# Block products with the tokens in the array, and a state space as real scans of states turned back by their angles

## The reference

```python
def s5_ssm(u, ...):                      # 32 groups of 16 channels, 64 complex states each
    bu_r, bu_i = einsum(uf, bbar_r), einsum(uf, bbar_i)          # bbar = coef * b
    x = associative_scan(_complex_scan_op, (a_r, a_i, bu_r, bu_i), axis=1)   # x_t = a x_{t-1} + bu_t
    return einsum(c_re, x_r) - einsum(c_im, x_i) + d * uf
def second_block(x, ...):
    for i in range(2):
        h = mixer_sb_ssm(x) if i == 0 else mixer_dsa(x)   # 0: stick-breaking attention beside s5_ssm, glu
        x = layer_norm_2(ALPHA * x + h)                   # 1: index scores, top-k mask, attention, 16 heads
        x = layer_norm_2(ALPHA * x + square(relu(x @ w1)) @ w2)              # 1024 -> 4096 -> 1024
```

## Time and profile before

| | us |
|---|---|
| median of 3 runs | 3764.23 (3763.64 to 3775.64) |
| the profiled execution | 3755.99 |
| its span | 3754.7 |
| TensorE, VectorE, ScalarE, GpSimd busy | 2697.8, 2004.3, 722.9, 1540.9 |
| the tail (from the first transpose of stage 1) | 2820 to 3754.7 |

### The profile page before, as it was taken

The page is one execution under the profiler, slowest core; times in us unless marked ns, Lnnn a source line. Parts: engine busy times, 40 slices in busy tenths (PEclk is TensorE's granted clock), DMA queues, the critical chain, the costliest instruction groups (busy, mean ns, idle before and its releaser), DMA issues.

```text
span 3754.7 us, 35721 instructions
## 1 busy us (share of the span) xinstructions
PE 2697.8 (72%) x12920; PEld 1223.2 (33%) x12920; DVE 2004.3 (53%) x5005; ACT 722.9 (19%) x1792; POOL 1540.9 (41%) x1632
## 2 busy tenths in 40 slices
PE   7758787787556775656697476565555499999998
PEld 2213332211112321111343121111114395766755
DVE  1156577745767677875213667777745655122311
ACT  0012212211122322211311121121112121020200
POOL 0034565554776666777100367767752000000000
PEclk9869988799877887776898687768887699999999
DMA  8578898899999999999432699999985268476657
GB/s 290 192 269 297 325 368 333 334 399 397 409 409 350 381 397 372 368 409 409 150 118 79 262 355 409 409 363 409 409 339 213 90 239 288 163 281 218 248 199 260
DMA packets 357508, 1145.99 MB, mean 305 GB/s; under 512 B 33412, under 2 KB 33668, under 8 KB 356308
## 3 DMA queue, kind: packets, MB, share of 16 engines
q0 software_dynamic: 236256, 867.34, 59.9%
q1 hardware_dynamic: 120660, 276.13, 20.5%
q10 hardware_dynamic: 416, 0.23, 0.0%
HBM read 1142.43 MB, written 1.15 MB: 305 GB/s over the span
## 4 chain that ended last, share of the span: by engine, by line
PE 45%; DMA 24%; DVE 17%; ACT 5%; POOL 5%; issue 3%; SPq 0%; DVEq 0%; ACTq 0%; POOLq 0%
DMA BIG<-in_p_u_dram,IDX 11%; PE PS L1012 9%; PE PS L1078 8%; DMA BIG<-in_p_v_dram,IDX 7%; DVE BIG L1873 6%; PE PS L1301 6%; PE PS L1283 5%; POOL BIG L2250 4%; DMA WR<-in_w_mod_dram 3%; PE PS L977 3%; PE PS L1040 2%; PE PS L1178 2%; PE PS L1272 2%; PE PS L988 1%; ACT dg L1468 1%
## 5 line engine op out<-in xcount | busy, mean ns | idle before, releaser
L1078 PE MATMUL PS<-BIG,dg 64*64 64x512 f32 x6144 | 1005.0, 784 | 669.0 <-DMA BIG<-in_p_v_dram,IDX 424.5
L2250 POOL DMA_INDIRECT BIG<-in_p_u_dram,IDX x768 | 737.7, 961 | 980.1 <-ACT PS L1455 463.1
L1873 DVE CUSTOM_DVE_ANT_0 BIG<-BIG,PS 128x1024 f32<-128x1024 f32 x768 | 930.3, 1216 | 322.3 <-DMA BIG<-in_p_u_dram,IDX 317.2
L2250 POOL DMA_INDIRECT BIG<-in_p_v_dram,IDX x768 | 734.3, 956 | 307.6 <-issue 136.0
L1078 PEld LDWEIGHTS PS<-BIG,dg 64*64 64x64 f32 x6144 | 263.0, 164 | 1327.9 <-issue 854.3
L1012 PE MATMUL PS<-WR,HT 128*128 128x512 f32 x640 | 300.9, 623 | 11.4 <-DMA WR<-in_b_w_in_dram 6.1
L1468 ACT ACTIVATE dg<-twin,ACTV 128x64 f32<-128x64 f32 x768 | 207.9, 336 | 330.0 <-PE PS L1078 220.7
L1283 PE MATMUL PS<-HT,WR 128*128 128x128 f32 x2048 | 258.3, 287 | 8.4 <-DMA WR<-in_mlp_w_dram 5.0
L1283 PEld LDWEIGHTS PS<-HT,WR 128*128 128x128 f32 x2048 | 248.1, 201 | 18.0 <-issue 6.2
L1301 PE MATMUL PS<-WR,BIG 128*128 128x512 f32 x512 | 227.3, 598 | 0.0
L977 PE MATMUL PS<-WR,scS 128*2 128x512 f32 x384 | 179.1, 620 | 38.9 <-DMA WR<-in_w_mod_dram 38.6
(11 more groups left out here) (295 smaller groups left out, 2730.8 us busy)
## 6 DMA issues: line engine op xcount, KB each, us to landing
WR<-in_mlp_w_dram SPq DMA_DIRECT2D x128, 1024.0 KB, 6.1
WR<-in_w_mod_dram SPq DMA_DIRECT2D x48, 1024.0 KB, 11.1
WR<-in_b_w_in_dram SPq DMA_DIRECT2D x18, 1024.0 KB, 9.6
WR<-in_a_w_in_dram SPq DMA_DIRECT2D x16, 1024.0 KB, 11.0
WR<-in_p_w_q_dram SPq DMA_DIRECT2D x16, 1024.0 KB, 9.4
BIG<-in_sb_ssm_w_in_dram POOLq DMA_DIRECT2D x16, 1024.0 KB, 7.5
BIG<-in_dsa_w_dram POOLq DMA_DIRECT2D x16, 1024.0 KB, 8.2
BIG<-in_p_u_dram,IDX POOLq DMA_INDIRECT x768, 9.4
```

Source lines behind the costliest of these rows:

```text
L1078: mm = self.e.matmul(pv[64 * i:64 * i + 64, 2 * r + n, :], dg[p, :], row[p, n * 512:n * 512 + 512], start=h == 0 and j == 0, stop=h == 7 a ...
L1873: self.e.tensor_tensor_reduce(row, row, xp, 1.0, 0.0, ALU.mult, ALU.add, m.ACTV[:, u % 4, j:j + 1]).then_inc(*self.done("dot", l, u, j))
L2250: self.e.indirect_dma_start(row, None, m.A[f"p_{table}"], bass.IndirectOffsetOnAxis(ap=m.IDX[:, u % 4, j:j + 1], axis=0)).then_inc(*m.GR.l ...
```

## The change

1. All projections but v go from `columns` to `rows_of` into a row tile (`RT`), and are transposed afterwards (`turn`: 4 transposes and a ScalarE copy). The index products of `dsa` likewise (`index_turn`).
2. `up`: the tokens in the array, four products of 512 columns for each half slab, two steps a slab, 16 steps in all. Relu on ScalarE, product with the PSUM rows on VectorE, and one slab later `up_turn`: 4 transposes and a copy. `down_begin` waits for the copy of the last slab, for `UP` has four banks now, and `DOWN` is two of them. Half slabs are freed singly.
3. The state space: tables of exp(-i angle t) for 64 steps (`turns`, once; a second table with the coefficients in it). `drive` multiplies the input by the table, so that the recurrence has only the real size |a|. `scan` is one `tensor_tensor_scan` for each state tile, part and chunk of 64 tokens (64 for a block); `scan_step` carries the state over the chunk, `unturn` multiplies back. `ssm_read` of group g waits for group g alone, and is now issued within `state_space`.
4. Side loads: k is asked for with the last drive product, and its slots are taken after v's: the order of `WB` is u, br, bi, q, v, k, cr, ci, glu, where k came before v. In `sb`, v's two slots are so br's and bi's, and k's are q's.

```diff
...
-        self.UP = Slots([PSt[:, 4 + i, :] for i in range(2)])
+        self.UP = Slots([PSt[:, 4 + i, :] for i in range(4)])
...
@@ -810,20 +812,15 @@
         self.flip(("sb", b), b, m.X[:, b, :])
         after = self.flipped(("sb", b), [b])
         yield
...
+            self.turns()
         self.side_slab(q, w, 0)
         yield
-        for j in range(16):
-            self.drive(b, j)
-            if j % 2:
-                yield
-        self.side_slab(k, w, 512)
-        yield from together(self.state_space(b), self.attention(b, q, k, v))
-        for c in range(4):
-            self.ssm_read(b, c)
-        yield
+        self.turn(u, m.s_u)
+        yield
+        yield from together(self.state_space(b, k), self.attention(b, q, k, v))
         for c in range(4):
             self.glu(b, c)
         yield
...
+    def state_space(self, b, k):
+        for g in range(4):
+            self.drive(b, g)
+            if g == 3:
+                self.side_slab(k, self.m.A["sb_ssm_w_in_2"][0], 512)
             yield
-        for c in range(1, 8):
-            self.carry_scan(b, c)
-            if c % 2:
-                yield
-        for n in range(15):
-            self.spread_scan(b, n)
+            self.scan(b, 0, g)
+        self.scan_step(b, 0)
+        for g in range(6):
+            if g < 4:
+                self.scan(b, 1, g)
+                self.unturn(b, g)
+            if g == 3:
+                self.scan_step(b, 1)
+            if g > 1:
+                self.ssm_read(b, g - 2)
             yield
     def attention(self, b, q, k, v):
         m, w = self.m, self.m.A["sb_ssm_w_in_2"][0]
-        self.columns(q, 4, self.block_of(b), m.a_q, ())
+        self.rows_of(q, self.block_of(b), None, ())
         self.side_slab(v, w, 1024)
         yield
-        self.columns(k, 4, self.block_of(b), m.a_k[:, :, b * 128:(b + 1) * 128], ())
+        self.turn(q, m.a_q)
+        yield from beats(3)
+        self.rows_of(k, self.block_of(b), None, ())
         self.side_one(("cr", b), m.A["s5_cr"])
         self.side_one(("ci", b), m.A["s5_ci"])
         yield
-        self.rows_of(v, self.block_of(b), m.a_v[:, :, b, :])
+        self.rows_of(v, self.block_of(b), m.a_v[:, :, b, :], ())
+        self.turn(k, m.a_k[:, :, b * 128:(b + 1) * 128])
         self.side_slab(("glu", b), m.A["ssm_w_glu_2"][0], 0, kts=4)
         yield
...
-                if n and j == 1:
-                    self.square(l, b, n - 1)
+            for half in range(2):
+                self.up(l, b, n, half, after)
+                if n and half:
+                    self.up_turn(l, b, n - 1)
                 yield
-        self.square(l, b, 7)
+        self.up_turn(l, b, 7)
...
         yield
         self.dsa_index(b)
+        yield
+        self.index_turn(b)
...
-            self.columns(("dsa", b, n), 4, self.block_of(b), dst, ())
+            self.rows_of(("dsa", b, n), self.block_of(b), None, ())
+            yield
+            self.turn(("dsa", b, n), dst)
             yield
...
+    def rows_of(self, slab, lhs, dst, after):
         m = self.m
         ps = m.PS.take("rows", slab)
-        self.wait_ge(*m.PS.emptied("rows", slab))
+        self.wait_ge(*after, *m.PS.emptied("rows", slab))
         for k in range(8):
             self.wait_ge(m.WB.landed(slab, k // 4))
             mm = self.e.matmul(ps, lhs(k), self.side_of(slab, k), start=k == 0, stop=k == 7)
...
+    def turn(self, slab, dst):
+        m = self.m
+        ps, rows = m.PS.take("turn", slab), m.RT.of(slab)
+        self.wait_ge(m.act.at("rows", slab), *m.PS.emptied("turn", slab))
+        for i in range(4):
+            mm = self.e.transpose(ps[:, i * 128:(i + 1) * 128], rows[:, i * 128:(i + 1) * 128], m.ident[:, :])
+        mm.then_inc(*self.done("turn", slab))
+        m.RT.free((slab,), self.done.last())
+    def drive(self, b, g):
+        m = self.m
         for i, name in enumerate((("br", b), ("bi", b))):
-            self.wait_ge(m.WB.landed(*name))
-            mm = self.e.matmul(ps[:, i * 128:(i + 1) * 128], cut(m.WB.of(*name), 16)[:, j, :], m.s_u[:, j // 4, :],
-                               start=True, stop=True)
-        mm.then_inc(*self.done("drive", b, j))
-        if j == 15:
-            for name in (("br", b), ("bi", b)):
+            ps = m.PS.take("drive", b, g, i)
+            self.wait_ge(m.act.at("turned", ("sb_in", b, 3)), m.WB.landed(*name), *m.PS.emptied("drive", b, g, i))
+            for k in range(4):
+                mm = self.e.matmul(ps[:, k * 128:(k + 1) * 128], cut(m.WB.of(*name), 16)[:, 4 * g + k, :],
+                                   m.s_u[:, g, :], start=True, stop=True)
+            mm.then_inc(*self.done("drive", b, g, i))
+            if g == 3:
                 m.WB.free(name, self.done.last())
...
         ps = m.PS.take("ssm", b, c)
-        self.wait_ge(m.dve.at("scanned", b), *m.PS.emptied("ssm", b, c))
...
+    def up(self, l, b, n, half, after):
         m, slab = self.m, ("w1", l, b, n)
-        ps = m.UP.of(l, b, n) if j else m.UP.take(l, b, n)
-        self.wait_ge(*after, *m.UP.emptied(l, b, n))
-        for k in range(8):
-            self.wait_ge(m.W.landed(slab, k // 4))
-            mm = self.e.matmul(ps[:, j * 128:(j + 1) * 128], m.slab_of(slab, k // 4)[:, k % 4, j * 128:(j + 1) * 128],
-                               m.HT[:, k, 256:384], start=k == 0, stop=k == 7)
-        mm.then_inc(*self.done("up", l, b, n, j))
-        if j == 3:
-            for k in range(2):
-                m.W.free((slab, k), self.done.last())
+        ps = m.UP.of("up", l, b, n) if half else m.UP.take("up", l, b, n)
+        self.wait_ge(*after, *m.UP.emptied("up", l, b, n), m.W.landed(slab, half))
+        for k in range(4):
+            mm = self.e.matmul(ps, m.HT[:, 4 * half + k, 256:384], m.slab_of(slab, half)[:, k, :],
+                               start=half == 0 and k == 0, stop=half == 1 and k == 3)
+        mm.then_inc(*self.done("up", l, b, n, half))
+        m.W.free((slab, half), self.done.last())
+    def up_turn(self, l, b, n):
+        m = self.m
+        ps, rows = m.UP.take("turn", l, b, n), m.RM.of(l, b, n)
+        self.wait_ge(m.dve.at("up", l, b, n), *m.UP.emptied("turn", l, b, n))
+        for i in range(4):
+            mm = self.e.transpose(ps[:, i * 128:(i + 1) * 128], rows[:, i * 128:(i + 1) * 128], m.ident[:, :])
+        mm.then_inc(*self.done("up turn", l, b, n))
+        m.RM.free((l, b, n), self.done.last())
...
-        self.wait_ge(*m.DOWN.emptied(l, b))
...
-        for g in range(3):
-            slab, c0, n = (v, 256 + g * 128, 512) if g < 2 else (i_, 0, 136)
+        for slab, n in ((("dsa_v", b), 512), (("dsa_i", b), 136)):
+            ps = m.PS.take("index", slab)
...
+            mm.then_inc(*self.done("index", slab))
...
+    def rows_of(self, slab, lhs, dst, after):
+        m, ps = self.m, self.m.PS.of("rows", slab)
+        if dst is None:
+            row = m.RT.take(slab)
+            self.wait_ge(m.pe.at("rows", slab), *m.RT.emptied(slab))
+            self.e.activation(row, ps, ACT.Copy).then_inc(*self.done("rows", slab))
+        else:
...
+    def up_turn(self, l, b, n):
+        m = self.m
+        self.wait_ge(m.pe.at("up turn", l, b, n))
+        self.e.activation(m.F[:, 4 * n:4 * n + 4, :], m.UP.of("turn", l, b, n).rearrange("p (f t) -> p f t", f=4),
+                          ACT.Copy).then_inc(*self.done("square", l, b, n))
+        m.UP.free(("turn", l, b, n), self.done.last())
...
+    def turns(self):
+        m = self.m
+        er, ei = m.turns
+        x, pr, pi = [m.s5c[:, 8 + i, :] for i in range(4)], m.s_turn[:, 0, :], m.s_turn[:, 1, :]
+        step = self.done.last(), self.done.last()
+        for n in (2, 4, 8, 16, 32, 64):
+            half = er[:, :, n // 2], ei[:, :, n // 2]
+            self.wait_ge(*step)
+            step = self.times(*half, *half, x, step, (pr, pi))
+            if n < 64:
+                t = [a[:, 0:16 * n].rearrange("p (j t) -> p j t", j=16) for a in m.s_t]
+                wr, wi = (p.unsqueeze(2).to_broadcast([128, 16, n]) for p in (pr, pi))
+                step = self.complex(er[:, :, n:2 * n], ei[:, :, n:2 * n], wr, wi, er[:, :, 0:n], ei[:, :, 0:n], t, step)
+        fr, fi = m.back
+        cr, ci = (m.s5c[:, i, :].unsqueeze(2).to_broadcast([128, 16, 32]) for i in (5, 6))
+        t = [a.rearrange("p (j t) -> p j t", j=16) for a in m.s_t]
+        for h in (slice(0, 32), slice(32, 64)):
+            step = self.complex(fr[:, :, h], fi[:, :, h], cr, ci, er[:, :, h], ei[:, :, h], t, step, conj=True)
+    def complex(self, outr, outi, pr, pi, sr, si, t, before, conj=False):
+        a = self.vf(outr, pr, sr, ALU.mult, *before)
+        b = self.vf(t[0], pi, si, ALU.mult)
+        c = self.vf(outi, pi, sr, ALU.mult)
+        d = self.vf(t[1], pr, si, ALU.mult)
+        return (self.vf(outr, outr, t[0], ALU.add if conj else ALU.subtract, a, b),
+                self.vf(outi, outi, t[1], ALU.subtract if conj else ALU.add, c, d))
...
```

(50 more changed lines are left out.)

214 lines of the change are left out of this document (76 added, 138 removed).

## The result

| | before | changed |
|---|---|---|
| median of 11 runs | 3768.70 (3757.17 to 3775.64) | 3783.39 (3778.79 to 3789.28) |
| ratio to before, 95% interval | | 1.0043 (1.0032 to 1.0055) |
| profiled execution | 3755.99 | 3787.3 |
| its span | 3754.7 | 3786.0 |
| start of the tail in it | 2820.04 | 2832.65 |

The kernel became slower by 0.43%; the median forecast was 3781, and 3783.39 lies inside the range. The two profiled executions differ by 31.3 us, more than the medians (14.7): 12.6 us of it lie ahead of the tail, where both issue the same instructions. The rest, 18.69 us, is the tail, and there the stages can be compared one by one. A stage is taken from the first transposes on TensorE to the next stage's.

What follows compares the result with a forecast made beforehand. TensorE bounds the kernel (45% of the chain); VectorE edits pay only in stage 1. Stage terms -19 + 5 + 12 + 13 + 6 = +17 us, on a median of 3764.2, gave 3781, range 3750 to 3806.

Steps and rivals of the forecast that it cites:

- Stage 1: Block 0 alone: shorter VectorE scan work, held back by late side loads, output product at 2954.5; -19 us.
- Rival B: Stage 1: k's load is not late and VectorE's chain alone ends it; -43 us, kernel 3757; chance 0.25 including a half case.
- Rival B's sign: Stage 1: the rival holds as soon as the k rows end before VectorE's third turn back (2900).
- The low end: Stage 1: no wait for loads and a short VectorE chain, output product at 2930; -43 us.
- Stage 2: Block 1 beside the first MLP: side-load waits and slow clock against mask waits that go; +5 us (-4 to +15).
- The norm before the heads: Stages 3 and 4: the MLP's norm stands on VectorE ahead of the last six heads' scores; +7.2 us each.
- The heads alone: Stages 3 and 4, heads without MLP beside them: VectorE's pace +4.1 and +3.1 us, TensorE's slow clock +4 and +5.
- my sums: Stages 3 and 4, top-k attention beside an MLP: all terms together +12 and +13 us.
- The stall before down: Before the first down product: TensorE idles about 1.7 us awaiting the last copy, with likely slow clock; +2.9 in stages 3 to 5.
- The order's size: Stages 3 and 4: MLP ends first; norm, heads' pace and slow clock cost, MLP slab waits of 6 and 5 us go.
- Wide up products: Each MLP: 512-column passes cost per column like narrow ones, plus transposes; +2.6 us, stage 5 +6 with the stall.
- Rival D: Interleaved stages: narrow passes lose more between other shapes, so wide ones win 0.7 us a slab; 3762; chance 0.06.

Runs made afterwards that it cites:

- e11: The changed kernel without the loads of k's and v's weights for block 0; ratio to the kernel before 1.0010.
- e6: The changed kernel with k's load issued ahead of v's; 3759.93 us, ratio to the kernel before 0.9986.
- e3: The kernel before with only its MLP steps cut to 32, narrow products kept; ratio to the kernel before 1.0047.
- e1: The changed kernel with 48 MLP steps restored, its wide up products in four steps a slab; ratio to the kernel before 1.0003.
- e5: The changed kernel run again unaltered, as a base on a second chip; ratio to the kernel before 1.0043.
- e7: The changed kernel with 48 MLP steps and Relu and its product issued one step later; ratio to the kernel before 1.0013.
- e8: The changed kernel with late norm, third top-k slab asked for early and k ahead of v; 3727.93 us, ratio to the kernel before 0.9895.
- e2: The changed kernel with the MLP's residual and norm 8 rounds later in stages 3 and 4; ratio to the kernel before 0.9987.
- e4: The changed kernel with the third top-k slab asked for one round sooner, ahead of the mask; ratio to the kernel before 1.0003.
- e10: The changed kernel with narrow up products, two steps a slab, late norm, early third top-k slab, k ahead of v; ratio to the kernel before 0.9875.

## Why the prediction was right, and where not

- **Stage 1, right for its reason.** TensorE waits 10.43 us for k, the first read 5.12 for the coefficients of the output. Tables took 21.8 us (2857.41 to 2879.2; 20 forecast), a drive and its scans 5.4 (5.3). Rival B's sign was badly chosen: the k rows did end (2911.9) before VectorE's third turn back began (2916.7), and the stage gained 17.6 us all the same, since the first read waited for its coefficients, whose slots only the k and v rows free. B needed the loads not to be late; even without any k and v loads (e11) the output product comes 24.7 us sooner than before, not 43. The low end was too low, because it let nothing else bind: e6 and e11 show the chain of drives, scans and reads on VectorE, then an attention that starts only behind it.
- **Stage 2, right sum, terms shifted.** My terms add up to +5.9, not +5. The loads cost 13.75 us of waits (11.34 + 1.11 + 1.30) where I had 8.5; with the slow clock behind them about 17 for 13.5. The wait for the mask went. What made up for the loads I had at 1 us: the wait before the output product fell from 6.28 to 1.98 us, and the product itself, at the fast clock now, from 16.19 to 14.00.
- **The norm before the heads, right.** 7.07 and 6.78 us idle, 7.2 forecast.
- **The heads alone, counted twice.** I added the heads' pace on VectorE (+4.1, +3.1) and the slow clock of TensorE (+4, +5). They don't add, for they are the same time: at 1.2 GHz a head of stage 3 takes TensorE 1.75 us, longer than VectorE's 1.31, and VectorE waits 0.54 us for TensorE at each head, so its own pace no longer shows. From the last product to the output product passed 19.2 us in stage 3; less the gap of 7.07 and the 7.0 of own work that is +5.1, not +8.1. In stage 4 it is 25.2 - 6.8 - 11.3 = +7.1, not +8.1.
- **The third top-k slab, missed.** I followed the side loads of `sb` in GpSimd's queue and not those of `dsa`. Two added steps put that load behind the mask: 4.6 us in stage 3; in stage 4 4.5 and 2.5 for the clock. In stage 4 it is more than the whole miss (16.1 for 13); in stage 3 it stands against the double count of 3 us.
- **What is then left.** With these two corrections my sums are 13.6 and 19.0 us, 3 more than measured in each stage. The stall before down is 1.2 of it: after it the clock stayed up in stages 3 and 4 (56 passes in 24.30 us), so it cost 1.7 us and not 2.9. Another 1.5 in stage 3 is a wait for a top-k slab that the kernel before had. The rest is within what a stage repeats to.
- **The order's size.** By my terms 32 steps in place of 48, with the slab waits that they end, cost 7.3 and 8.3 us in stages 3 and 4. e3, which makes that edit alone, shows 6.4 and 3.6.
- **Wide up products, right.** +2.6 for the products and 2.9 for the stall were forecast for the last MLP. Of the 5.4 measured, 1.7 is the stall's idle time (0.97 + 0.69), 1.8 the slow clock in the down products behind it (56.90 us for 55.10), and 1.9 is left for products and transposes. I gave the fall of the clock half a chance; in stage 5 it came in the changed kernel, e1, e5, e6, e7, e8 and e11 and not in e2 and e4. The changed kernel's down products, the clock just behind the stall (the 0.64 in the row), and e2's down products:

```profile
3719.31 56.90 PE L1307 MATMUL PS<-WR,BIG 128*128 128x512 f32 x128 [0.69 <-ACT BIG L1637]
```

```profile
3719.30:3724.00 4.70, 4.69 (x7) 0.64 0.34 139
```

```profile
3874.55 55.20 PE L1309 MATMUL PS<-WR,BIG 128*128 128x512 f32 x128 [0.69 <-ACT BIG L1639]
```

- **Rival D fell.** Narrow passes between other shapes do not lose enough: e10, which has them, has a shorter tail than e8.
- **Against the profiled execution the sum was right (+17 for +18.69); for the medians the difference is 14.7.** Part of the closeness is luck: a double count of 3 us and a missed wait of 4.6 stood against each other, a single stage repeats only to 2.4 us, and 3781 was counted from a median of 3764.2, which became 3768.7 with more runs.

What stays open: how much of e8's and e10's gain in a single stage is the clock, since whether it fell differed between runs of the same code; why the ratios of e1, e3 and e11 differ from their tails; and stage 1's 16.5 us wait for the tables, which no run took away.

## What to carry to other kernels

Where streams take turns step by step, a change in how many steps one stream has moves everything behind it in every engine's queue. Count the steps of each stream before and after, and then follow every wait and every load issue across the ones that it has passed: here a norm ahead of heads, a load behind a mask and a load behind one whose slot is freed later were worth 51 us of tail (953.3 to 902.1), while the whole change had lengthened it by 19. When an engine comes out of an idle stretch into work that it shares with another, price its slow clock and its partner's pace as the longer of the two, not as their sum.

## What was not expected of the hardware

- GpSimd's `affine_select` on 128x512 elements, the same instruction at the same place, took 11.73 us in the kernel before and 17.94 in e3, while VectorE ran the scan's two-input operations back to back, and 0.64 in the changed kernel, where VectorE waits for TensorE or ScalarE beside it. VectorE's stream alone does not settle it: the other three selects of stage 1 in the kernel before (2887.91, 2915.59 and 2923.58) took 0.78, 0.66 and 0.64 us in the middle of the same scan, and beside each one VectorE operation took some 0.3 to 0.4 us longer than its like; the same happened at the very end of the 11.73 us (0.78 us for 0.39 at 2907.16). The rows are of the kernel before, of e3 and of the changed kernel:

```profile
2895.98 11.73 POOL L2290 TENSOR_SCALAR_AFFINE_SELECT H<-H 128x512 f32<-128x512 f32 x1 [7.29 <-ACT H L1601]
```

```profile
3064.54 17.94 POOL L2291 TENSOR_SCALAR_AFFINE_SELECT H<-H 128x512 f32<-128x512 f32 x1 [7.32 <-ACT H L1602]
```

```profile
2947.84 0.64 POOL L2346 TENSOR_SCALAR_AFFINE_SELECT H<-H 128x512 f32<-128x512 f32 x1 [3.19 <-ACT H L1602]
```

  The 6.2 us between the first two go with e3's longer stage 1 (179.6 for 174.2). No run isolates it, and none shows why one select was held and its neighbours were not. The page SBUF — State Buffer of the Trainium skill (section on SBUF's two separate sides) has VectorE and GpSimd share a pair of ports as an exclusive lock, held for a whole instruction, when a VectorE operation has two inputs in SBUF; the rows agree in that one of the two is held up each time, but one VectorE operation there lasts 0.4 us and the select took over 11, so if this is the lock, the select lost it to many of them in a row.
- The scan's 0.19 us for 64 elements stands between the starts of 64 elements (0.14) and 128 (0.20) of an ordinary two-input operation in the same trace, near the latter. That is nearly half the throughput; the page DVE: opcode table, instruction layouts, handler registers and perf-mode slots of the Trainium skill (6, on feedback) has half for this scan, and the trace agrees.
